# Value-page rounds of a gate unit issued as one pair at k 10 instead of singly at k 6 and k 18

## What is computed

```python
y_conv = (zb * y_c) @ w_conv_out                 # branch A
y_diff = o.reshape(B, T, V_W) @ w_diff_out       # branch B, o = sum over keys of (p1 - lam*p2) * v
y_mem  = mem_attn(qm, mem_k, mem_v) @ w_cross_out  # branch C
g = sigmoid(zg.reshape(B, T, 3, D_MODEL))        # D_MODEL = 2048
merged = g[:, :, 0] * y_conv + g[:, :, 1] * y_diff + g[:, :, 2] * y_mem
x = x + merged @ w_o
# a sample token reads its past from 16 pages of 128 rows, 8 heads of 128 values each:
v_past = cache_v[page_table].reshape(8, 2048, 8, 128)
```

## Time and profile before

| | |
|---|---|
| time, median of 3 runs | 2716.74 us (2715.25 to 2717.34) |
| the profiled execution, its own time | 2717.42 us |
| its span, first to last instruction | 2715.7 us |
| PE busy | 2428.8 us, 89% |
| DVE busy | 1488.8 us, 55% |
| POOL busy | 913.6 us, 34% |
| ACT busy | 349.5 us, 13% |
| read from and written to memory | 338 GB/s over the span |
| mean granted clock of PE | 0.973 |

### The profile page before, as it was taken

The page is one execution under the profiler, slowest core; times in us unless marked ns, Lnnn a source line. Parts: engine busy times, 40 slices in busy tenths (PEclk is TensorE's granted clock), DMA queues, the critical chain, the costliest instruction groups (busy, mean ns, idle before and its releaser), DMA issues.

```text
span 2715.7 us, 27186 instructions
## 1 busy us (share of the span) xinstructions
PE 2428.8 (89%) x8845; PEld 1510.8 (56%) x8845; DVE 1488.8 (55%) x2386; ACT 349.5 (13%) x773; POOL 913.6 (34%) x889
## 2 busy tenths in 40 slices
PE   9999999999999999999996777777999597777777
PEld 7888886488666688888883223332434142222333
DVE  3599996732222240012587787875555556554543
ACT  2111000022222210001112110111101011111100
POOL 1122220101222200000157565564553565445542
PEclk9999999999999999999998999998889899999999
DMA  7699995865899945456589999999999999999998
GB/s 228 224 400 386 384 369 215 305 217 183 310 366 351 356 136 196 159 173 217 207 319 389 416 417 414 417 418 421 421 404 421 406 414 419 413 422 417 419 421 369
DMA packets 269444, 919.24 MB, mean 338 GB/s; under 512 B 16154, under 2 KB 122738, under 8 KB 200308
## 3 DMA queue, kind: packets, MB, share of 16 engines
q0 software_dynamic: 122448, 725.64, 66.2%
q1 hardware_dynamic: 133156, 164.93, 18.1%
q10 hardware_dynamic: 13728, 27.26, 2.7%
HBM read 909.08 MB, written 8.72 MB: 338 GB/s over the span
## 4 chain that ended last, share of the span: by engine, by line
PE 52%; DMA 24%; DVE 11%; POOL 6%; issue 5%; ACT 0%; DVEq 0%; POOLq 0%; ACTq 0%; SPq 0%
PE ps L807 13%; PE ps L699 13%; DMA sb_bregion<-in_peer_u_dram,sb_ring 11%; PE ps L819 6%; PE ps L1057 5%; DMA sb_mkv<-in_peer_u_dram,sb_ring 4%; PE ps L689 4%; PE ps L794 4%; DMA sb_S<-in_peer_u_dram,sb_ring 3%; DVE sb_bregion L2031 3%; PE ps L908 2%; DMA sb_wring<-in_w_in_dram 2%; DVE sb_mkv L2031 2%; POOL sb_bregion L558 1%; DMA sb_bregion<-in_peer_v_dram,sb_ring 1%
## 5 line engine op out<-in xcount | busy, mean ns | idle before, releaser
L1057 PE MATMUL ps<-sb_wring,sb_ring 128*128 128x512 f32 x992 | 453.5, 606 | 86.8 <-DMA sb_wring<-in_peer_v_dram,sb_ring 85.7
L2031 DVE CUSTOM_DVE_ANT_0 sb_bregion<-sb_bregion,sb_rows 128x2048 f32<-128x2048 f32 x128 | 293.5, 2293 | 219.1 <-DMA sb_bregion<-in_peer_u_dram,sb_ring 212.1
L699 PE MATMUL ps<-sb_hT,sb_wring 128*128 128x264 f32 x1792 | 407.6, 388 | 1.2 <-DMA sb_wring<-in_w_in_dram 1.0
L1057 PEld LDWEIGHTS ps<-sb_wring,sb_ring 128*128 128x128 f32 x992 | 185.1, 193 | 353.3 <-issue 257.5
L699 PEld LDWEIGHTS ps<-sb_hT,sb_wring 128*128 128x128 f32 x1792 | 338.6, 191 | 59.8 <-DMA sb_wring<-in_w_in_dram 2.8
L807 PE MATMUL ps<-sb_hT,sb_wring 128*128 128x264 f32 x1536 | 365.6, 389 | 1.1 <-DVEq L1418 1.1
L807 PEld LDWEIGHTS ps<-sb_hT,sb_wring 128*128 128x128 f32 x1536 | 286.4, 190 | 64.1 <-issue 16.4
L1057 PE MATMUL ps<-sb_oreg,sb_ring 128*128 128x512 f32 x496 | 237.3, 629 | 76.8 <-DMA sb_oreg<-in_peer_v_dram,sb_ring 56.7
L1057 PE MATMUL ps<-sb_hT,sb_ring 128*128 128x512 f32 x496 | 231.9, 614 | 56.3 <-DMA sb_hT<-in_peer_v_dram,sb_ring 48.6
L558 POOL DMA_INDIRECT sb_bregion<-in_peer_u_dram,sb_ring x132 | 182.6, 1383 | 213.2 <-DVEq L1418 170.7
L1385 ACT ACTIVATE sb_ring<-sb_ident,sb_ring 128x128 f32<-128x128 f32 x248 | 99.6, 402 | 924.5 <-PE ps L1057 786.7
(11 more groups left out here) (367 smaller groups left out, 2581.8 us busy)
## 6 DMA issues: line engine op xcount, KB each, us to landing
sb_wring<-in_w_in_dram SPq DMA_DIRECT2D x26, 2048.0 KB, 11.8
sb_ring<-in_cache_k_dram POOLq DMA_DIRECT2D x64, 512.0 KB, 8.1
sb_mkv<-in_cache_k_dram POOLq DMA_DIRECT2D x64, 512.0 KB, 8.5
sb_wring<-in_w_in_dram SPq DMA_DIRECT2D x26, 1024.0 KB, 12.1
sb_wring<-in_w_in_dram ACTq DMA_DIRECT2D x26, 1024.0 KB, 13.3
sb_mkv<-in_cache_v_dram POOLq DMA_DIRECT2D x48, 512.0 KB, 7.3
sb_rows<-in_cache_v_dram POOLq DMA_DIRECT2D x47, 512.0 KB, 7.8
sb_wring<-in_w_mem_kv_dram SPq DMA_DIRECT2D x8, 2048.0 KB, 9.8
```

What stands on the lines that cost most here:

```text
L699: last = mm(ps[:, c, 0:NT], whalf[:, h, k % BC, c * P:(c + 1) * P], rhs[:, k, :], start=(k == 0), stop=(k == KC - 1))
L1057: last = mm(ps[:, 4 * t + q, :], diag[:, k % 4, :], e_slots[v % ER][:, q * 512:(q + 1) * 512], start=False, stop=q_stop, skip_group_check= ...
L2031: st(V.tensor_tensor_reduce(out=u_slots[n % UR], in0=u_slots[n % UR], in1=h2, scale=1.0, scalar=0.0, op0=ALU.mult, op1=ALU.add, accum_out= ...
```

## The change

In units 11 to 26 both value rounds are issued behind the product k 10, one directly behind the other. `columns` of the odd units from 13 on moves from k 12 to k 10 and stands ahead of the two rounds. Nothing is added or removed, and only PE's program is touched.

```diff
                 if 8 <= q < 12 and k == 10:
                     columns(q, q - 8)
-                if 11 <= q < 27 and k in (6, 18):
-                    value_round(MEM_ROUNDS + 2 * (q - 11) + k // 18)
-                if 13 <= q < 29 and q % 2 and k == 12:
+                if 13 <= q < 29 and q % 2 and k == 10:
                     columns(q, MEM_ROUNDS + (q - 13) // 2)
+                if 11 <= q < 27 and k == 10:
+                    for n in range(2):
+                        value_round(MEM_ROUNDS + 2 * (q - 11) + n)
```

## The result

| | before | changed |
|---|---|---|
| time, median of 11 runs each on the same chip | 2716.73 us (2712.47 to 2719.73) | 2723.49 us (2719.39 to 2725.3) |
| ratio, 95% interval | | 1.0027 [1.0018, 1.0035] |
| the profiled execution, its own time | 2717.42 us | 2724.5 us |
| its span | 2715.7 us | 2722.8 us |
| start of unit 11 to start of unit 27 | 256.30 us | 265.23 us |

The changed kernel is slower, by 6.8 us between the medians; the interval is 4.9 to 9.5 us. The two starts in the last row are those of the first gate product of the unit: 705.17 and 961.47 before, 704.09 and 969.32 after.

A forecast was written before the change was run, and what follows sets the result against it. The prediction took PE's own instruction stream to bound the stage. Seams -5.3, waits at `columns` +11.7 and the first pair's page wait +1.7 gave +8.1 us: median 2724.8 us, range 2718.5 to 2731.

The forecast's parts named there:

- Part 1, the seams: PE, switching between products and value rounds: 0.31 us saved in 16 units, 0.04 more in eight odd ones; gain 5.3 us.
- Part 2, the waits at `columns`: Odd units 13 to 25: PE waits for late `sums_added`, five times 1.8 us and twice 1.35; loss 11.7 us.
- Part 3, the first pair: Unit 11's second round, now reached sooner, waits for its fourth page: loss 1.7 us, bounds 1 and 2.5.
- signs that the prediction named for being wrong: DVE at `mask_sums` by U + 2 (U: odd unit's start), page waits in later units, or round pairs over 3.7 us.
- the own range: Whole-kernel time for the forecast case, from the bounds other than that of the seam: 2720.5 to 2728.5 us.
- Nothing is waited for: Rival: PE's stream gets shorter without waits at `columns`; 2713.1 us, chance 0.08; part-way case 2718 to 2722, another 0.10.
- The pages come too late: Rival: bursts of eight page loads reach the next unit's second round late, 3 to 8 us more, near 2730; chance 0.12.
- G + 5.74: Even units: DVE ends `normalise` 5.74 us behind G, the start of the first branch product, also after the change.

The follow-up runs named there:

- changed, again: The changed kernel unaltered, run once more on another occasion: 2724.35 us, ratio 1.0032 against the kernel before.
- unit 11 kept: Against the changed kernel, unit 11 alone has its value rounds back behind products 6 and 18: 2721.52 us, ratio 1.0028 to the kernel before.
- only even paired: Against the changed kernel, odd units go back to rounds at k 6 and k 18, `columns` at k 12: 2721.07 us, ratio 1.0022 to the kernel before.
- columns alone: Against the changed kernel, rounds go back behind products 6 and 18; `columns` stays at product 10: 2714.85 us, ratio 0.9999 to the kernel before.
- columns behind the pair: Against the changed kernel, `columns` goes back behind product 12, the pair stays behind product 10: 2713.75 us, ratio 0.9995 to the kernel before.
- exponentials first: Against the changed kernel, ScalarE makes the exponentials ahead of the sigmoid from unit 12 on: 2713.73 us, ratio 0.9996 to the kernel before.
- spread further: Against the kernel "spread", the odd pair moves behind product 14 and `columns` behind product 16: 2714.34 us, ratio 0.9998 to the kernel before.
- only odd paired: Against the changed kernel, even units go back to rounds at k 6 and k 18: 2714.12 us, ratio 0.9994 to the kernel before.
- spread: Against the changed kernel, the odd units' pair moves behind product 12 and `columns` behind product 14: 2712.82 us, ratio 0.9992 to the kernel before.

## Why the prediction was right

The prediction was +8.1 us, 2724.8; measured were +6.8 and, on the second occasion, +9.1 us. Both intervals hold 8.1, but they are 4.6 and 6.8 us wide, so that the whole time alone would not tell a forecast of 8.1 from one of 6 or 9. The profiled executions differ outside the stage too, where the program is the same: unit 11 starts between 704.09 and 708.04 us in them. So the parts of the forecast are held against the stage:

| | stage, us | against before | waits of PE for VectorE | for pages |
|---|---|---|---|---|
| changed | 265.23 | +8.93 | 10.3 | 0.8 |
| changed, again | 264.00 | +7.70 | 10.3 | 1.2 |
| unit 11 kept | 262.84 | +6.54 | 10.3 | 0 |
| only even paired | 262.17 | +5.87 | 7.9 | 0 |
| columns alone | 256.30 | 0.00 | 0 | 0 |
| columns behind the pair | 255.85 | -0.45 | 0 | 3.5 |
| exponentials first | 255.02 | -1.28 | 0 | 3.6 |
| spread further | 254.59 | -1.71 | 0 | 2.9 |
| only odd paired | 253.56 | -2.74 | 0 | 0.4 |
| spread | 253.55 | -2.75 | 0 | 1.6 |

**Part 1, the seams: -5.3, measured -5.8.** Two pairs save 0.63 us in "Spread", so 0.315 each against the 0.31 forecast; the even units of the changed kernel, at 15.92 us (720.95 to 736.87) for 16.24, say the same. Two rounds behind each other show no seam (1.72). `columns` next to a pair saves 0.10 in the odd unit (0.41 - 0.31 in "Only odd paired"), where I counted 0.04: moved alone it saves nothing, so what it saves comes of standing at the round. 16 x 0.315 + 8 x 0.10 = 5.8.

**Part 2, the waits at `columns`: +11.7, measured +11.9.** Two units from one wait to the next take 33.28 us (809.61 to 842.89), forecast 33.3. Without a wait they would take 32.18 - 0.31 - 0.41 = 31.46, so a wait costs 1.82 (forecast 1.8). Here two small errors cancel: the chain from the merge to the end of `mask_sums` took 4.37 us (838.31 to 842.68) instead of 4.47, and signal and restart took 0.28 instead of 0.15, 0.21 until `columns` starts and 0.07 until the round behind it does (0.29 behind `columns`, for 0.22 without a wait in "Exponentials first"). The list of waits has only 1.59 of the 1.82, since it counts from the end of the last product and not from its step. In unit 15, 776.31 - 743.48 = 32.83 gives 1.37 (forecast 1.35). Unit 13 lasts 17.00 us (736.87 to 753.87) and would last 15.95 - 0.41 = 15.54, so its wait costs 1.46. 5 x 1.82 + 1.37 + 1.46 = 11.9. The mechanism is shown from three sides: "Only even paired" has the lateness without the moved `columns`, "Columns alone" the moved `columns` without the lateness, and "Exponentials first" both moves of PE with a chain that is no longer late, and no wait.

**Part 3, the first pair: +1.7, measured 1.0 and 1.25.** In the profile of the changed kernel the fourth page was issued 1.87 us behind the start of unit 11, as before (1.86), but landed in 6.5 us instead of 7.3. PE came to the second round 7.5 us into the unit (709.86 + 1.72 = 711.58), as forecast. The list has 0.81 us of idleness, under the 1 to 2.5 that I gave for it. Unit 11 lasts 16.86 us (704.09 to 720.95); it lasted 16.27 and would have saved 0.41, so the wait costs 1.0. On the second occasion PE idled 1.06 and unit 11 lasts 17.11: 1.25. There the 0.15 in unit 15 makes that unit 0.3 us longer as well, and it is one of the signs that the prediction named for being wrong, a page wait in a later unit, though a small one.

**The sum.** The first profile: -5.8 + 11.9 + 1.0 = +7.1, and the 1.8 us of the clock (below), which no step of the forecast had: +8.9, measured +8.93. The second: -5.8 + 11.9 + 1.25 + 0.3 = +7.7, measured +7.70. "Unit 11 kept" has neither unit 11's wait nor its saving: -5.8 + 0.4 + 11.9 = +6.5, measured +6.54. So the terms account for the stage. Without the clock the forecast's 8.1 was 1.0 and 0.4 us too high: the seams half a microsecond too small, the page half a microsecond or more too large. That 8.1 also lies between the two measured medians is luck as far as these tenths go. One sum of the prediction is off: its bounds add up to 2721.7 to 2727.0, and the own range was given as 2720.5 to 2728.5.

**The rivals.** *Nothing is waited for* fell with the first list of waits. "Exponentials first" makes its condition true, and there VectorE is waited for no more; but the page waits that the rival had at 1.7 us are 3.6 then, so that its stage gains 1.3 and not 3.6. *The pages come too late* was not what the changed kernel does, but was not wrong either. Its arithmetic (the fifth page of a burst of eight, on the way from an even pair to an odd one, 8.7 us to land) is what "Columns behind the pair" shows: PE is through with the first round at 807.06 + 1.72 = 808.78, 8.7 us behind the issue at 800.05, and the page took 9.5. What kept it small in the changed kernel is the cushion that the prediction names, the wait for `columns` ahead of the round. The two losses are not added but stand one behind the other: taking the first away lets 2.2 to 2.5 us of the second appear in the later units, beside unit 11's, which is why undoing the late `normalise` brings the kernel back to even and not 5 us under it.

**Is there a better version?** "Spread" (2712.82, -2.5 us, [0.9983, 1.0001]) and "Only odd paired" (-1.2 us) have the shortest stages, 2.7 us shorter than before, 0.1% of the kernel. But "Columns behind the pair" and "Exponentials first" have medians 1.6 us lower than before with stages that are only 0.5 and 1.3 shorter, so differences of this size are not told apart by the whole time, and the intervals of all four reach 1: none is shown to be faster than the kernel before. The seams are worth 5 us, and the waits for pages take 2.3 ("Spread") to 4.6 us ("Columns behind the pair") of them back where all units are paired.

## What to carry to other kernels

When work on the bounding engine is pulled forward from between two points, ask which other engine used that stretch: a value round between branch products was also the time in which ScalarE and VectorE finished the unit's softmax, and closing the gap on one engine opened a wait on the same engine in the next unit. Count from the event that starts the other engine's chain (G + 5.74) and not from where its result is used, and count every unit in which it holds. And a wait can hide a second one behind it, so the worth of removing it is what the next one leaves; pairing work that frees buffers also pairs the refills, so that those at the end of the burst are asked for later; here it was the fifth page of a burst that PE came to wait for.

## What the runs showed of the hardware that was not expected

**Half clock behind a wait, once.** In the first profile of the changed kernel, windows of PE behind the wait that ends at 842.89 (us, busy time of PE, PEld, DVE, ACT, POOL, clock, DMA share, GB/s):

```profile
840.00:842.00 2.00, 1.30 (x6) 0.76 (x4) 1.85 (x2) 1.44 (x2) 0.00 (x0) 1.00 1.03 402
842.00:844.00 2.00, 1.08 (x6) 0.45 (x10) 0.85 (x2) 0.00 (x0) 0.00 (x0) 0.84 1.04 411
844.00:846.00 2.00, 2.00 (x16) 0.58 (x12) 0.00 (x0) 0.00 (x0) 0.00 (x0) 0.50 0.90 352
846.00:848.00 2.00, 2.00 (x19) 0.43 (x12) 0.00 (x0) 0.00 (x0) 0.00 (x0) 0.80 0.04 16
...
809.61:842.89 33.28, 31.70 (x182) 21.64 (x182) 8.90 (x18) 6.79 (x15) 8.46 (x16) 1.00 0.96 345
842.89:877.96 35.07, 33.46 (x181) 22.03 (x182) 8.90 (x18) 6.79 (x15) 8.46 (x16) 0.95 0.92 329
```

The granted clock was 0.50 (1.2 GHz) for some 3 us of value rounds and 1.00 (2.4 GHz) before and after; the two units took 1.79 us more than their neighbours. PE had been idle for 1.58 us ahead of it, but it had been idle for 1.58 or 1.59 ahead of four other `columns` too, with the clock at 1.00 in the windows behind them, and in the second profile of the same kernel the same units took 33.28 us with a clock of 1.00:

```profile
846.55:879.83 33.28, 31.69 (x182) 21.64 (x182) 8.90 (x18) 6.79 (x15) 8.49 (x16) 1.00 0.98 346
```

The seven waits of "Unit 11 kept" had no such stretch behind them either, and the clock is 1.00 throughout this stage in the profiles of the kernel before and of every other run. So the idleness stood ahead of the lower clock once, and nothing here shows that it caused it; what else it takes is open.

**Landings grow within a burst.** In "Columns behind the pair" the eight pages of a burst, issued 1.16 to 1.46 us apart from 795.39 on, landed in 7.3, 7.9, 8.4, 8.9, 9.5, 9.3, 9.4 and 9.5 us, and in "Spread further" five in 8.4, 8.9, 9.4, 9.9 and 10.5: in "Spread further", and in the first five of the other row, a page lands about 1.7 us behind the one ahead of it, though it was issued 1.16 behind it. This is not a price of pairing alone: in the kernel before, four pages issued from 921.30 on landed in 8.1, 8.4, 8.9 and 9.5 us. Nor is it the same in every burst: the next one of "Columns behind the pair", from 810.15 on, took 4.4, 5.6, 6.0, 6.1, 6.2, 6.4, 6.5 and 7.0 us. Pairing makes bursts of eight where there were bursts of four, and what a place further back costs differs from burst to burst.
